# Attention scores of two heads at once on the halves of TensorE's rows, and softmax jobs of two chunks with both heads

## The reference, cut to what matters

```python
# first: 16 query heads, 2 key heads, blocks of 128 queries see this block and the one before
s = einsum('bnqkgd,bnskd->bnkgqs', qb, kb) * scale + alibi      # masked outside the window
m = maximum(max(s), sink); p = exp(s - m); p = p / (sum(p) + exp(sink - m))
o = einsum('bnkgqs,bnskd->bnqkgd', p, vb)
# second: 8 query heads, 2 key heads, blocks see the block before, this one and the next (<= 384 keys)
# third: 8 heads, each query sees 16 columns of all 8 rows of a grid of 8 x 64 tokens, with a bias table:
sc = einsum('bchd,brckhd->bhcrk', qr, kn) * scale + bias; p = softmax(sc); o = einsum('bhcrk,brckhd->bchd', p, vn)
```

## Time and profile before

| | before |
|---|---|
| time, median of 3 runs | 1233.96 us |
| the profiled execution's own time | 1234.33 us |
| its span, first to last instruction | 1232.5 us |
| PE busy | 1203.5 us, 98% |
| DVE busy | 643.3 us, 52% |
| ACT busy | 524.1 us, 43% |
| POOL busy | 167.8 us, 14% |
| mean granted clock of TensorE | 0.991 |

### The profile page before, as it was taken

How to read it: one execution, slowest core, us unless ns; L and a number is a source line. 1 busy time by engine, 2 the same in 40 slices (tenths; PEclk the granted TensorE clock), 3 DMA queues, 4 the chain that set the end, 5 groups by cost and what they waited for, 6 DMA issues and landing times.

```text
span 1232.5 us, 14352 instructions
## 1 busy us (share of the span) xinstructions
PE 1203.5 (98%) x5318; PEld 945.0 (77%) x5318; DVE 643.3 (52%) x1083; ACT 524.1 (43%) x905; POOL 167.8 (14%) x215
## 2 busy tenths in 40 slices
PE   8999989999999999999999999999999999999995
PEld 5777767787776778787887777887788888888884
DVE  6787877743557665455444444546444232444221
ACT  6657746542555544233434343325433121433222
POOL 1022113220213212222111110003000000000011
PEclk9999998999999999999999999999999999999997
DMA  5322222432111123311222212232223323223211
GB/s 208 104 86 86 86 86 69 131 103 69 35 35 52 35 69 102 97 58 52 69 71 76 86 60 86 86 102 88 101 86 102 100 89 99 90 86 103 86 52 69
DMA packets 29878, 103.08 MB, mean 84 GB/s; under 512 B 3312, under 2 KB 3568, under 8 KB 29808
## 3 DMA queue, kind: packets, MB, share of 16 engines
q1 hardware_dynamic: 29376, 101.37, 25.3%
q10 hardware_dynamic: 432, 0.79, 0.2%
HBM read 100.05 MB, written 2.10 MB: 83 GB/s over the span
## 4 chain that ended last, share of the span: by engine, by line
PE 91%; DVE 4%; ACT 3%; issue 1%; DMA 1%; POOL 0%; SPq 0%; DVEq 0%; ACTq 0%; POOLq 0%
PE ps L665 26%; PE ps L667 26%; PE ps L666 25%; PE ps L804 2%; PE ps L828 2%; PE ps L771 2%; PE ps L831 1%; PE ps L779 1%; PE ps L837 1%; PE ps L792 1%; DVE cc L1277 1%; ACT wh L868 1%; PE ps L719 1%; DMA xt<-xT 1%; PE ps L737 1%
## 5 line engine op out<-in xcount | busy, mean ns | idle before, releaser
L665 PE MATMUL ps<-xgh,wh 128*128 128x512 f32 x848 | 374.4, 442 | 3.4 <-DVE wl L1170 2.9
L667 PE MATMUL ps<-xgh,wl 128*128 128x512 f32 x848 | 336.1, 396 | 0.0
L666 PE MATMUL ps<-xgl,wh 128*128 128x512 f32 x848 | 336.0, 396 | 0.0
L1170 DVE TENSOR_TENSOR wl<-raw,wh 128x1024 fp32r<-128x1024 f32 x180 | 230.2, 1281 | 154.9 <-ACT wh L868 154.8
L868 ACT ACTIVATE wh<-raw 128x1024 fp32r<-128x1024 f32 x180 | 188.3, 1048 | 134.3 <-PE ps L667 134.3
L665 PEld LDWEIGHTS ps<-xgh,wh 128*128 128x128 f32 x848 | 159.7, 188 | 48.3 <-issue 14.7
L666 PEld LDWEIGHTS ps<-xgl,wh 128*128 128x128 f32 x848 | 159.8, 188 | 40.6 <-issue 6.9
L667 PEld LDWEIGHTS ps<-xgh,wl 128*128 128x128 f32 x848 | 159.3, 188 | 37.9
L1047 ACT ACTIVATE Pt<-Pt,stat 128x256 f32<-128x256 f32 (+2 forms) x128 | 64.9, 507 | 140.9 <-DVE stat L1380 55.9
L1660 POOL TENSOR_SCALAR Pt<-Pt,stat 128x256 f32<-128x256 f32 (+2 forms) x128 | 71.1, 568 | 338.8 <-DVE stat L1412 241.9
L667 PE MATMUL ps<-fh,wl 128*128 128x512 f32 x256 | 102.1, 399 | 0.0
(11 more groups left out here) (231 smaller groups left out, 1683.1 us busy)
## 6 DMA issues: line engine op xcount, KB each, us to landing
raw<-wst SPq DMA_DIRECT2D x180, 512.0 KB, 3.5
bst<-nbias SPq DMA_DIRECT2D x8, 256.0 KB, 2.6
xt<-xT SPq DMA_DIRECT2D x3, 512.0 KB, 8.0
outT<-ot SPq DMA_DIRECT2D x6, 256.0 KB, 3.0
raw<-wst SPq DMA_DIRECT2D x2, 256.0 KB, 4.0
outT<-ot ACTq DMA_DIRECT2D x2, 256.0 KB, 2.7
cstt<-cst SPq DMA_DIRECT2D x1, 448.0 KB, 5.7
selt<-sel SPq DMA_DIRECT2D x1, 320.0 KB, 4.2
```

The source lines that it names most:

```text
L665: e.matmul(o, high, a, start=(k == 0), stop=False)
L666: e.matmul(o, high, b, start=False, stop=False)
L667: e.matmul(o, low, a, start=False, stop=stop).then_inc(tile_done, 1)
L1170: e.tensor_tensor(wl_t[:, u % NHL, :], raw_t[:, u % NRAW, :], f32(wh_t[:, u % NHL, :]), ALU.subtract).then_inc(lo_done, 1)
```

## The change

- **Scores.** The two heads of a chunk are computed by two matmuls of 64 rows each, one on partitions 0 to 63 into bank 3, one on 64 to 127 into bank 4. Both stand at the step of the first; the step of the second is empty. The pair waits until both scores of the pair before have been read.
- **Jobs.** A job holds both heads of two chunks (two blocks of queries in "n") instead of one head of four. `half` takes the place of p, and the order of the heads in bias, sink and tables follows (`head`).
- **Products.** In the first attention one matmul of 512 columns becomes two of 256 (one for each parity, into the half of the bank of the job's chunks). In the second there are two of 256 as before, now split by parity. In the third the four of a block of keys alternate between partitions 0 to 63 and 64 to 127 of the bank.
- **Keys.** The copies need no zeros any more: `ke` has two instead of four tiles, `kea` two instead of four, `kb_t` four instead of eight. The 16 memsets on POOL, and the waits for them, are gone. The third attention's keys are written by one operation of 128 partitions for each chunk.
- **Bias tables.** Four buffers instead of two; four of the transfers are issued at the start, and the other four when the jobs with the chunk that used the buffer have read it.

```diff
+        for c in range(4):
+            for half in range(2):
+                jobs.append(dict(kind="n", c=c, half=half, k0=0, nk=2))
...
+        def head(job, i):
+            return {"s": 8 * job.get("g", 0) + 4 * job["half"] + i, "w": 4 * job["half"] + i, "n": 2 * job.get("c", 0) + i % 2}[job["kind"]]
...
                 for h in range(8):
-                    yield end["z", 7] if h < 2 else step_at["score", 24 + h - 2, 3] + 1.0
-                    if h >= 2:
-                        q.wait_ge(bias_done, 4 * (24 + h - 2) + 4)
+                    last_use = 24 + 2 * (h // 2 - 2) + 1
+                    yield end["z", 7] if h < 4 else step_at["score", last_use, 3] + 1.0
+                    if h >= 4:
+                        q.wait_ge(bias_done, 4 * last_use + 4)
...
             def scores(kind):
                 for m in range(*SETS[kind][:2]):
                     job = jobs[m]
-                    for i in range(4):
+                    for i in (0, 2):
                         yield step_at["score", m, i]
                         x = 4 * m + i
-                        q.wait_ge(bias_done, x - 1)
-                        o = bank[SB[x % 2]]
...
-                            e.matmul(o[:, 0:w], q1[:, 4 * g + i, blk(n)], ke[g][p][:, keys(job)], start=True,
-                                     stop=True).then_inc(score_done, 1)
...
+                        q.wait_ge(bias_done, x)
+                        a = 2 * job["half"] + i // 2
+                        for p, r in ((0, lo), (1, hi)):
+                            o = bank[SB[p]]
+                            if kind == "s":
...
+                                own, seen = q1[r, 4 * g + a, blk(job["n"])], ke[g][r, keys(job)]
...
+                            e.matmul(o[:, 0:128 * job["nk"]], own, seen, start=True, stop=True).then_inc(score_done, 1)
...
             def prods(kind):
...
-                        if kind == "s":
-                            g = job["g"]
-                            done = e.matmul(bank[PV], padded(V1, job["k0"] + kb, g, p), src, start=first and p == 0, stop=final and p == 1)
...
-                            for i in range(4):
-                                done = e.matmul(grid_block(bank[PV][r, :], i), Vb[:, key_block(i, kb), 64 * h:64 * h + 64],
-                                                src[:, blk(i)], start=first and i == 0, stop=final and i == 3)
+                        first, final = kb == 0 and half == 0, kb == job["nk"] - 1 and half == 1
+                        if kind == "n":
+                            for i in range(2):
+                                a = 2 * half + i
+                                for p, r in ((0, lo), (1, hi)):
+                                    h = 2 * job["c"] + p
+                                    done = e.matmul(grid_block(bank[PV][r, :], a), Vb[:, key_block(a, kb), 64 * h:64 * h + 64],
+                                                    src[:, blk(2 * i + p)], start=first and i == 0, stop=final and i == 1)
+                        else:
+                            v = V1 if kind == "s" else Va
+                            for p in range(2):
+                                done = e.matmul(bank[PV][:, 256 * half:256 * half + 256], padded(v, job["k0"] + kb, job["g"], p),
+                                                src.rearrange("p (c h t) -> p c h t", c=2, h=2)[:, :, p, :], start=first and p == 0,
+                                                stop=final and p == 1)
```

More of the change, by code:

```diff
@@ L242, in build @@
         q1 = sb("q1", [128, KD, S], F, ph)
-        ke = [[sb(f"ke{g}{p}", [128, S], F, ph)[:, :] for p in range(2)] for g in range(2)]
+        ke = [sb(f"ke{g}", [128, S], F, ph)[:, :] for g in range(2)]
         V1 = sb("V1", [128, 1088], F, ph)
@@ L264, in build @@
         qa = sb("qa", [128, 4, S], F, ma)
-        kea = sb("kea", [128, 4, S], F, ma)
+        kea = sb("kea", [128, 2, S], F, ma)
         ma.close()
         mg = sb("mg", [128, KD, S], F, ph)
-        bst = [sb(f"bst{i}", [128, 2, 256], F, qk) for i in range(2)]
+        bst = [sb(f"bst{i}", [128, 2, 256], F, qk) for i in range(4)]
         Pt2 = [sb(f"Pt2{i}", [128, 384], F, qk)[:, :] for i in range(8)]
@@ L294, in build @@
         par_in, cst_in, cst2_in, sel_in = (sem(n) for n in ("par_in", "cst_in", "cst2_in", "sel_in"))
-        bias_in = [sem(f"bias_in{i}") for i in range(2)]
+        bias_in = [sem(f"bias_in{i}") for i in range(4)]
         out_done = sem("out_done")
@@ L399, in build @@
                 k0 = max(0, n - 1)
-                for p in range(2):
-                    jobs.append(dict(kind="s", g=g, n=n, p=p, k0=k0, nk=n + 1 - k0))
+                for half in range(2):
+                    jobs.append(dict(kind="s", g=g, n=n, half=half, k0=k0, nk=n + 1 - k0))
         for n in range(NBLK):
             k0, k1 = max(0, n - 1), min(NBLK, n + 2)
[L404 to L407, removed]
+            for half in range(2):
+                jobs.append(dict(kind="w", g=half, n=n, half=half, k0=k0, nk=k1 - k0))
+        for c in range(4):
+            for half in range(2):
+                jobs.append(dict(kind="n", c=c, half=half, k0=0, nk=2))
         for m, job in enumerate(jobs):
@@ L809, in prods @@
                     job = jobs[m]
-                    p = job["p"]
-                    r = (lo, hi)[p]
+                    half = job["half"]
                     for kb in range(job["nk"]):
@@ L1077, in outs @@
                     else:
-                        e.activation(ybh[:, job["h"] // 2, :], bank[PV], ACT.Copy).then_inc(o_done, 1)
+                        e.activation(ybh[:, job["c"], :], bank[PV], ACT.Copy).then_inc(o_done, 1)
             def eighth():
@@ L1377, in biases @@
                         if kind == "s":
-                            h = 8 * job["g"] + 2 * i + job["p"]
+                            h = head(job, i)
                             bias = D1 if job["n"] else D1[:, 128:256]
@@ L1382, in biases @@
                         elif kind == "w":
-                            h, a0 = 2 * i + job["p"], (job["k0"] - job["n"] + 1) * 128
+                            h, a0 = head(job, i), (job["k0"] - job["n"] + 1) * 128
                             e.tensor_tensor_reduce(pa[:, 0:w], sa, D2[:, a0:a0 + w], -SL2[h], drvc(NSK2 + h, NSK2 + h + 1), ALU.add,
@@ L1386, in biases @@
                         else:
-                            h = job["h"]
-                            q.wait_ge(bias_in[h % 2], 16 * (h // 2) + 16)
-                            e.tensor_tensor_reduce(pa[:, 0:w], sa, bst[h % 2][:, i // 3, :], -1.0, BIG, ALU.add, ALU.min,
+                            h = head(job, i)
+                            q.wait_ge(bias_in[h % 4], 16 * (h // 4) + 16)
+                            e.tensor_tensor_reduce(pa[:, 0:w], sa, bst[h % 4][:, (2 * job["half"] + i // 2) // 3, :], -1.0, BIG, ALU.add, ALU.min,
                                                    neg).then_inc(bias_done, 1)
@@ L1401, in biases @@
                             es = stat_(m, 2, i - 1, i + 1)
-                            sa = PAR["sinks"][0] + 8 * job["g"] + job["p"] if kind == "s" else PAR["sink2"][0] + job["p"]
+                            sa = PAR["sinks" if kind == "s" else "sink2"][0] + head(job, i)
                             q.wait_ge(bias_done, x + 1)
-                            e.tensor_tensor(es, stat_(m, 0, i - 1, i + 1), part[:, sa + 2 * (i - 1):sa + 2 * i + 1:2],
+                            e.tensor_tensor(es, stat_(m, 0, i - 1, i + 1), part[:, sa - 1:sa + 1],
                                             ALU.add).then_inc(es0_done, 1)
```

100 lines of the change are left out of this document (31 added, 69 removed).

## The result

The changed kernel takes 1225.03 us (median of six runs, 1223.90 to 1227.12) against 1234.49 for the kernel of before on the same chip: -9.5 us, a ratio of 0.9925 with the 95% interval 0.9912 to 0.9938. Forecast were 1239.7 and slower. The time lies in the range (1224 to 1251), at its lower end, and where the first rival put it (1224); the direction was wrong.

The account below looks back on a forecast made before the run. PE (TensorE) was taken to bound the kernel. The terms +24.3 - 13.8 - 5.3 + 0.5, rest 0, gave +5.7 on the profiled 1234.33, 1240.0; as that run lay 0.4 above the median, 1239.7 us; 8-in-10 range 1224 to 1251.

Parts of the forecast that it names:

- the first rival: Score pairs and third attention's products: halves run fully together, -9.8 us, 1224; chance 0.16, a third for scores alone.
- Part 1: Score pairs: each of 64 pays two changes of array shape at 0.19 us, none hidden, +24.3 us; lower bound 0.
- Part 2: Score pairs: four passes take three pass times, saving a quarter, -13.8 us; bounds 0 and -27.6.
- Part 3: Products: third attention's groups take five pass times instead of eight, -5.3 us, bounds 0 and -7.0; first two attentions 0.
- Part 4: PE's waits for bias reads, as a pair needs both banks: +0.5 us; bounds -0.9 and 14 us.
- Part 5: The rest: dropped zeroing on POOL, joined DVE operations and bias table transfers change nothing, 0 us.
- Both passes side by side: The first rival: halves fully together in score pairs (-27.6) and third attention's products (-7.0), 1224 us; chance 0.16.
- Changes cost nothing: Changes of array shape around the score pairs are free: -18.6 us, 1215; chance 0.05.
- column halves no: Score pairs overlap on row halves, but the third attention's products don't on column halves: +11.0 us, 1245; chance 0.18.
- f32 halves don't run together: Neither score pairs nor products overlap in f32, while changes of shape are paid: +24.8 us, 1259; chance 0.13.
- The two-bank wait decides: First attention: some 10 pairs lose 0.5 us each waiting for both banks, +10.7 us, 1245; chance 0.06.

Follow-up runs that it names:

- e3_split: The changed kernel with the second score of each pair at a step of its own again; 1266.1 us, ratio 1.0255 to the kernel of before.
- e4_group: The changed kernel with all four scores of a job at once in the 28 jobs of at most 256 columns; 1215.75 us, ratio 0.9859 to the kernel of before.
- e2_prod_order: The changed kernel with the third attention's products ordered head lo's two blocks first, then head hi's; 1225.91 us, ratio 0.9934 to the kernel of before.
- e1_same_half: The changed kernel with both matmuls of every score pair on rows 0 to 63; 1249.91 us, ratio 1.0125 to the kernel of before.
- e5_columns: The changed kernel with the first two attentions' products as 64-column halves without zero padding; 1220.10 us, ratio 0.9889 to the kernel of before.
- e7: The changed kernel with the first two attentions' products in 64-column halves and all products of a job at its last step; 1210.22 us, ratio 0.981.
- e8_all: The edits of e7 and e4_group together on the changed kernel; 1206.58 us, ratio 0.9776 to the kernel of before.
- e9_early_bias: e8_all with the second attention's scores in pairs again and later softmax steps two slots earlier on DVE, ACT and POOL; 1203.78 us, ratio 0.975.

## Why the prediction was wrong

**Part 1, changes of shape: right.** Forecast +24.3 (0.38 a pair). The rows of e3_split give 0.39, and a pair of the changed kernel has the open load on both sides; e4_group took half of the changes of 28 jobs away and got 9.3 us, with 10.6 for the changes less 1.9 of waits expected by these prices.

**Part 2, what the pair saves: the failed step.** It said "A2 uses the rows of A1 and waits for it; B1 can then start with A2", three pass times, -13.8. The pair takes two, -27.6. The step leaned on "in the whole trace matmuls start in their order in the queue". That was read from rows in which each matmul used the half, or the whole, that the one ahead of it used, or (in the gates) where the lists of both halves alternate anyway, so that it couldn't tell order in the list from order in a half. The bound of part 2 was right and the choice within it wrong. The rule of the Trainium skill quoted there, that matmuls start and end strictly in program order, does not hold for these matmuls on different halves: in e2_prod_order a matmul starts ahead of a whole one that stands before it in the list. Its other rule (TensorE: Matmul & The Clock Gate, Part 3: Packing small matmuls), that a pack lasts one matmul and a few ns, agrees: 0.45 for a pair's four passes, where one head's two took 0.43.

**Part 3, products: mechanism right, size too small by the same step.** Forecast -5.3 (five pass times). L831's groups show four: from L673 to L672 behind the group 683.22 - 681.96 = 1.26 us

```profile
681.96 0.40 PE L673 MATMUL ps<-yah,wl 128*128 128x512 f32 x1
...
683.22 0.39 PE L672 MATMUL ps<-yal,wh 128*128 128x512 f32 x1
```

and before 1.68 (the 1.91 of the earlier trace rows to the L667, less 0.235). 0.42 x 16 = -6.7. No cost in the first two attentions, as said: the second keeps its 80 passes, the first has 112 of 256 columns.

**Part 4, waits: under-sized.** Forecast +0.5; PE's waits on the bias passes rose from 0.9 to 3.4 us (two that sum to 2.0 and one of 1.4 in the rows under e4_group): +2.5, above the 2 us that the prediction gave as its sign. The one of 1.4 is at the start of the second attention, which the part didn't look at. The grace that the part counted on didn't cover it; no run shows how large such a grace is.

**Part 5: right.** POOL has 16 instructions fewer and 8.3 us less work, DVE 5.4 us less, and PE has no new wait on them. Its wait on POOL's scaling in the first attention fell from 1.4 to 0.6 us; whether that came with the memsets or with the new jobs is not shown.

**The sum again.** +24.3 - 27.6 - 6.7 + 2.5 = -7.5; measured -9.5 in the medians (-10.9 to -7.7 by the interval of the ratio), and -8.5 in the three attentions of the traces. By stage, against the kernel of before: in the first attention +12.2 for changes, -12.1 for passes (24 pairs of 256 columns, 8 of 128) and +0.5 for PE's idle time as a whole (3.5 us before, 3.9 after, since the wait on POOL's scaling fell while those on the bias passes grew) are +0.5, and measured is +0.2. In the second +6.1 - 8.6 + 1.4 = -1.1, measured -1.2. In the third +6.1 - 6.9 - 6.7 = -7.5, measured -7.5. That makes -8.1 against -8.5; the -7.5 of the terms lies just outside the interval of the medians. The same prices (0.38 for a pair of changes, 0.215 for a pass of 256 columns, and PE's idle time as the trace has it: 2.1 us in the first attention of e1_same_half, 1.5 in e3_split, 5.1 in e4_group) give the experiments, as differences to the changed kernel:

| worked out, measured | first | second | third |
|---|---|---|---|
| e1_same_half | +10.2, +9.7 | +7.7, +7.7 | +6.9, +6.8 |
| e3_split | +15.3, +14.1 | +13.3, +13.3 | +13.0, +13.0 |
| e4_group | -4.9, -5.1 | -0.7, -0.7 | -3.0, -3.1 |

In the second and third attention they meet within 0.1 us. In the first they come out 0.2 to 1.2 too high, most in e3_split; why stays open.

**Rivals.** "Both passes side by side" held, at 1224. "Changes cost nothing", "column halves no" and "f32 halves don't run together" are excluded by e3_split, e5_columns and e1_same_half. "The two-bank wait decides": the wait was real and small.

## What to carry to other kernels

Work on part of the matrix engine's rows or columns between full-size matmuls pays a toll at each change (0.38 us in and out here), whatever its own length; so count the stretches before the saving, and gather small work until one stretch is worth several tolls. One pair of 128 columns between dense tiles loses (0.38 for 0.22), one of 256 breaks even (0.38 for 0.43), groups of four win (e4_group). For the two halves to run together, their matmuls needed no alternation in the list, at least with two of one half ahead of the other's.

When a forecast hangs on one choice between two bounds with opposite signs of the sum (here -13.8 or -27.6 against +24.3), a row that shows the order only where both readings agree decides nothing; the chances should then be nearer to even than 0.42 + 0.18 to 0.16.

## What the runs showed of the hardware

- A matmul on one half of the array starts ahead of matmuls on the other half that stand before it in the list, by at least one whole f32 matmul and one pass (e2_prod_order: 0.67 us for eight passes, as with alternation).
- Plain f32 passes on two row halves (0.45 us for four of 256 columns) and on two column halves (e7: twelve passes of 256 columns in 1.52 us, one behind the other they would be 12 x 0.215 = 2.6) run at full overlap, each half with its own moving data.
- A change of shape costs the same for 64 rows in f32 as for the gates' faster type: 0.39 for two here, 0.19 for one in the earlier trace rows. For 64 columns it is 0.33 for two.
- The granted clock fell to its lower level, 1.2 GHz, as a wait of PE between busy stretches ended: 0.89 over 15 us with a wait of 2.2 us (e8_all), 0.55 over 7.5 us with one of 1.9 (e9_early_bias). In e4_group a wait of 2.2 had no such cost.
